# Stick-breaking attention with queries on partitions, a running product along keys, and weights transposed by DMA

## The reference

```
mask = s_idx[None, :] < t_idx[:, None]
log_keep = jnp.where(mask, jax.nn.log_sigmoid(-z), 0.0)
log_stick = lax.cumsum(log_keep, axis=3, reverse=True) - log_keep
w = jnp.where(mask, jnp.exp(jax.nn.log_sigmoid(z) + log_stick), 0.0)
outs.append(jnp.einsum('bhqk,bhkd->bhqd', w.astype(v.dtype), vb))
```

## Time and profile before

| | us |
|---|---|
| runs of the kernel | 2827.84, 2835.94 and 3204.79; median 2835.94 |
| span of the profiled execution, slowest core (core 1) | 2821.7 |
| spans of the 8 cores in it | 2811.3 to 2821.7 |
| what lies around the span: median less span | 14.2 |
| what lies around the span: lowest run less span | 6.1 |

### The profile page before, as it was taken

The page is one execution under the profiler, slowest core; times in us unless marked ns, Lnnn a source line. Parts: engine busy times, 40 slices in busy tenths (PEclk is TensorE's granted clock), DMA queues, the critical chain, the costliest instruction groups (busy, mean ns, idle before and its releaser), DMA issues.

```text
span 2821.7 us, 37239 instructions; the slowest of 8 cores (2811.3 to 2821.7 us)
## 1 busy us (share of the span) xinstructions
PE 2501.4 (89%) x12740; PEld 1036.7 (37%) x12740; DVE 1023.9 (36%) x1602; ACT 1201.3 (43%) x1559; POOL 69.6 (2%) x88
## 2 busy tenths in 40 slices
PE   3988788788999899999998888778899999999993
PEld 1433232222444344444444332222234444444441
DVE  3223232222344543343442332222233364343343
ACT  4346778787223211111343576788842231111132
POOL 0000000000000000000000000000000000000000
PEclk9999798888999999999999998888899999999997
DMA  6110020000222222205002001100022433330202
GB/s 160 16 16 1 1 31 1 1 1 12 27 38 38 45 46 45 46 1 77 1 1 31 1 1 19 12 1 1 1 28 33 53 45 45 45 44 12 36 30 90
DMA packets 79829, 79.81 MB, mean 28 GB/s; under 512 B 4128, under 2 KB 65696, under 8 KB 79648
## 3 DMA queue, kind: packets, MB, share of 16 engines
q0 software_dynamic: 69696, 60.54, 15.6%
q1 hardware_dynamic: 9952, 16.89, 1.8%
HBM read 129.57 MB, written 8.39 MB: 49 GB/s over the span
## 4 chain that ended last, share of the span: by engine, by line
PE 80%; ACT 8%; DVE 4%; DMA 4%; issue 3%; ACTq 0%; DVEq 0%; SPq 0%; POOLq 0%
PE psb L245 58%; PE psb L252 20%; ACT BW L261 5%; PE psb L248 3%; DMA X<-xT 2%; ACT L261 1%; DVE MIX L264 1%; DMA yT<-BW 1%; DVE BW L277 1%; ACT FW L261 1%; DVE H L267 1%; DVE BW L274 0%; DMA WB<-w_in 0%; DVE MIX L274 0%; DMA WB<-w_out 0%
## 5 line engine op out<-in xcount | busy, mean ns | idle before, releaser
L261 ACT ACTIVATE FW<-psb 128x512 f32<-128x512 f32 (+7 forms) x509 | 370.8, 742 | 932.0 <-PE psb L245 795.8
L245 PE MATMUL psb<-H,MIX 128*128 128x512 bf16 (+1 forms) x3168 | 630.7, 358 | 0.5 <-DVE MIX L264 0.3
L252 PE MATMUL psb<-BW,CST 128*128 128x512 bf16 (+5 forms) x1352 | 381.5, 399 | 38.4 <-DVE BW L264 38.4
L245 PEld LDWEIGHTS psb<-H,MIX 128*128 128x128 bf16 x3168 | 286.0, 98 | 336.7 <-issue 7.5
L252 PE MATMUL psb<-MIX 64*128 64x512 bf16 (+5 forms) x1424 | 274.0, 389 | 127.7 <-ACT BW L261 123.0
L261 ACT ACTIVATE BW<-psb 128x1024 bf16<-128x1024 f32 (+5 forms) x424 | 354.8, 904 | 52.3 <-PE psb L252 50.4
L264 DVE TENSOR_TENSOR X<-X,psb 128x512 f32<-128x512 f32 (+1 forms) x504 | 307.9, 629 | 146.3 <-PE psb L245 145.7
L245 PE MATMUL psb<-MIX 128*128 128x512 bf16 (+1 forms) x1584 | 327.9, 357 | 31.8 <-DVE MIX L264 31.5
L264 DVE TENSOR_TENSOR BW<-BW 128x1024 bf16<-128x1024 bf16 (+2 forms) x320 | 195.5, 611 | 367.9 <-PE psb L252 211.2
L245 PE MATMUL psb<-H,WB 128*128 128x512 bf16 (+1 forms) x1472 | 313.5, 364 | 1.3 <-ACT FW L261 0.8
L264 DVE TENSOR_TENSOR MIX<-FW,psb 128x512 bf16<-128x512 f32 (+1 forms) x198 | 124.1, 630 | 452.4 <-PE psb L245 449.3
(11 more groups left out here) (47 smaller groups left out, 1140.2 us busy)
## 6 DMA issues: line engine op xcount, KB each, us to landing
MIX<-w_ffn_in POOLq DMA_DIRECT2D x20, 1024.0 KB, 14.0
MIX<-w_ffn_out POOLq DMA_DIRECT2D x10, 1024.0 KB, 22.4
X<-xT SPq DMA_DIRECT2D x4, 2048.0 KB, 35.1
WB<-w_in POOLq DMA_DIRECT2D x8, 1024.0 KB, 20.0
yT<-BW SPq DMA_DIRECT2D x32, 256.0 KB, 2.5
WB<-w_in POOLq DMA_DIRECT2D x12, 512.0 KB, 8.5
WB<-w_out POOLq DMA_DIRECT2D x4, 1024.0 KB, 10.9
BW<-w_in POOLq DMA_DIRECT2D x4, 512.0 KB, 9.6
```

Source lines behind the costliest of these rows:

```text
L245: P.op('pe', lambda e: e.matmul(out, lhsT=lhsT, rhs=rhs, start=start, stop=stop), reads, writes, inc)
L252: P.op('pe', lambda e: e.matmul(out, lhsT=lhsT, rhs=rhs, start=start, stop=stop, skip_group_check=True), reads, writes, inc)
L261: P.op('act', lambda e: e.activation(out=out, in_=in_, func=func, **kw), reads, writes)
```

## The change

Tokens are laid out in reversed order (the host reverses x and the learned tokens, and reverses the output back), so that keys before a query lie to the right of it. Attention is written anew with queries on partitions. A unit is one head, one block of 128 queries and up to eight key blocks. For each unit TensorE computes z (one or two matmuls of up to 457 columns, and a mask on the diagonal), ScalarE computes sigmoid(-z) into float32, which is 1 - beta, VectorE runs `tensor_tensor_scan` along the keys, which leaves the running product, and subtracts neighbouring columns of it, which gives the weights in bf16. A longer key prefix is cut into two or three chunks, and one column of the product is copied as the start of the next. Then the SP queue transposes the weights block by block with `dma_start_transpose`, SBUF to SBUF, and TensorE multiplies them with V, for two query blocks and two heads together.

Softplus, Exp, the second z, the triangular matmul and the running sum go. The tiles WB, BW and FW become parts of one tile ATT, which attention uses whole. So k and v are projected for all tiles before attention, and the first merge slab is loaded after it. There are 232 units in the first layer and 224 in the second.

```diff
@@ token order and key blocks @@
-TT = [(0, 16)] + [(16 + 512 * i, 16 + 512 * (i + 1)) for i in range(4)]
-KB = [(0, 16)] + [(16 + 128 * j, 144 + 128 * j) for j in range(16)]
+TT = [(512 * i, 512 * (i + 1)) for i in range(4)] + [(2048, 2064)]
+KB = [(128 * j, 128 * j + 128) for j in range(16)] + [(2048, 2064)]
...
@@ memory: one tile ATT now holds what WB, BW and FW were @@
-        FW = sb("FW", 2048, F32)
+        ATT = sb("ATT", 20480, BF16)
-        WB = sb("WB", 4 * 2048, BF16)
-        BW = sb("BW", 8192, BF16)
+        WB, BW, FW = Sub(ATT, 0), Sub(ATT, 8192), Sub(ATT, 16384, 2)
+        P.alias = dict(WB=('ATT', 0, 1), BW=('ATT', 8192, 1), FW=('ATT', 16384, 2))
...
@@ attention: all of the former body removed @@
-        def attention(work=None, after_work=None, ft=0):
...
+        def chunks(b):
+            n = 17 - b
+            nch = 1 if n <= 8 else 2 if n <= 15 else 3
+            cuts, k = [], b
+            for c in range(nch):
+                m = -(-(17 - k) // (nch - c))
+                if c < nch - 1:
+                    m = min(m, 7)
+                cuts.append((k, k + m))
+                k += m
+            return cuts
+
+        def attention(l, ft=0):
+            KE0, WR0, WT0 = 0, 6144, 10240
+            memset('dve', MIX[:, 8256:8272], 0.0, [('MIX', 8256, 8272)])
+            memset('pool', ATT[:, WR0:WR0 + 4096], 0.0, [('ATT', WR0, WR0 + 4096)])
+            units, nch, npo = [], 0, 0
+            for g in ([8] if ft == 0 else []) + list(range(7, -1, -1)):
+                bs = [16] if g == 8 else [2 * g, 2 * g + 1]
+                for hp in range(4):
+                    chs = chunks(bs[0])
+                    for ci, (ka, kz) in enumerate(chs):
+                        ch = dict(bs=bs, hp=hp, ka=ka, kz=kz, first=ci == 0, last=ci == len(chs) - 1,
+                                  wt=WT0 + (nch % 2) * 4096, po=6 + npo % 2)
+                        nch += 1
+                        for bi, b in enumerate(bs):
+                            lo = max(ka, b)
+                            if lo >= kz:
+                                continue
+                            for hh in range(2):
+                                units.append(dict(ch=ch, bi=bi, b=b, hh=hh, lo=lo, end=False, n=len(units)))
+                        units[-1]['end'] = True
+                    npo += 1
+
+            def geo(u):
+                k0, k1 = KB[u['lo']][0], KB[u['ch']['kz'] - 1][1]
+                return k0, k1, k1 - k0 + 2, KB[u['b']][1] - KB[u['b']][0]
+
+            def ke(u):
+                return KE0 + (u['n'] % 3) * 2048
+
+            def zap(u, nq, W):
+                T_ = PSB[u['n'] % 3]
+                if W <= 512:
+                    return T_[0:nq, 0:W]
+                return T_[0:nq, :].rearrange("p (h c) -> p h c", h=2)[:, :, 0:W // 2]
+
+            def prep(u):
+                k0, k1, W, nq = geo(u)
+                ch, hp, hh = u['ch'], u['ch']['hp'], u['hh']
+                q0 = KB[u['b']][0]
+                T_, zb = PSB[u['n'] % 3], 2 * (u['n'] % 3)
+                p0, p1 = 64 * hh, 64 * hh + 64
+                diag = u['lo'] == u['b']
+                parts = [(0, W)] if W <= 512 else [(0, W // 2), (W // 2, W)]
+                mw = min(NMSK, W)
+                for x, (a, b_) in enumerate(parts):
+                    msk = diag and x == 0
+                    mmx(T_[0:nq, x * 512:x * 512 + b_ - a], Q.ap(hp, q0, q0 + nq, p0, p1),
+                        K.ap(hp, k0 - 2 + a, k0 - 2 + b_, p0, p1), True, not msk,
+                        [Q.r(hp, q0, q0 + nq), K.r(hp, k0 - 2 + a, k0 - 2 + b_)], [psr(zb + x)], not msk)
+                    if msk:
+                        mmx(T_[0:nq, 0:mw], CST[0:nq, 0:nq], CST[0:nq, 128:128 + mw], False, True,
+                            [r_cst], [psr(zb)], True)
+
+            def core(u):
+                k0, k1, W, nq = geo(u)
+                ch = u['ch']
+                L = W - 2
+                kb_ = ke(u)
+                r_ke = ('ATT', kb_, kb_ + 2 * W)
+                E = ATT[0:nq, kb_:kb_ + 2 * W].bitcast(F32)
+                out = E if W <= 512 else E.rearrange("p (h c) -> p h c", h=2)
+                zb = 2 * (u['n'] % 3)
+                act(out, zap(u, nq, W), AF.Sigmoid, [psr(zb)] + ([psr(zb + 1)] if W > 512 else []), [r_ke],
+                    scale=-1.0)
+                cs = u['bi'] * 2 + u['hh']
+                init = 1.0 if u['lo'] == u['b'] else CAR[0:nq, cs:cs + 1]
+                r_car = ('CAR', cs * 16, cs * 16 + 16)
+                P.op('dve', lambda e: e.tensor_tensor_scan(
+                    out=E, data0=E, data1=ZF[0:nq, 0:1].to_broadcast([nq, W]), initial=init,
+                    op0=ALU.mult, op1=ALU.add),
+                    [r_ke, ('ZF', 0, 16)] + ([] if u['lo'] == u['b'] else [r_car]), [r_ke])
+                if not ch['last']:
+                    cp('dve', CAR[0:nq, cs:cs + 1], E[:, W - 3:W - 2], [r_ke], [r_car])
+                wo = WR0 + (u['n'] % 4) * 1024
+                r_w = ('ATT', wo, wo + 1024)
+                tt(SUBE, ATT[0:nq, wo:wo + L], E[:, 1:L + 1], E[:, 2:L + 2], ALU.subtract, [r_ke], [r_w])
+                nb = ch['kz'] - u['lo']
+                wt = ch['wt']
+                W4 = ATT[:, wt:wt + 4096].rearrange("p (k h q) -> p k h q", h=2, q=256)
+                i0 = u['lo'] - ch['ka']
+                qc = u['bi'] * 128
+                dst = W4[:, i0:i0 + nb, u['hh'], qc:qc + nq]
+                src = ATT[0:nq, wo:wo + nb * 128]
+                wr = [('ATT', wt + (k * 2 + u['hh']) * 256 + qc, wt + (k * 2 + u['hh']) * 256 + qc + nq)
+                      for k in range(i0, i0 + nb)]
+                P.dma('sp', lambda e: e.dma_start_transpose(out=dst, in_=src), 'tw%d' % (u['n'] % 4), [r_w], wr)
+
+            def av(ch):
+                hp, po, wt = ch['hp'], ch['po'], ch['wt']
+                for kb in range(ch['ka'], ch['kz']):
                     b0, b1 = KB[kb]
+                    nk = b1 - b0
+                    i0 = kb - ch['ka']
+                    N = sum(KB[b][1] - KB[b][0] for b in ch['bs'] if b <= kb)
+                    st_ = ch['first'] and i0 == 0
+                    sp_ = ch['last'] and kb == ch['kz'] - 1
                     for hh in range(2):
...
@@ the order of a layer @@
             ecnt = [0]
-            if ft == 0:
-                proj_fm(l, 0, 0, 'q')
-            proj_fm(l, 1, 0, 'q')
-            for i in range(5):
+            for i in (4, 3, 2, 1, 0):
+                if i in tl:
+                    proj_fm(l, i, 0, 'q')
                 proj_u(l, i, 2, ecnt)
-                if i + 2 < 5:
-                    proj_fm(l, i + 2, 0, 'q')
-                if i == 2:
-                    load_in_slab(l, 512, 0)
-                if i >= ft:
+                if i in tl:
                     pool_band(l, i)
+            load_in_slab(l, 512, 0)
             load_in_slab(l, 1024, 2)
-            for i in range(2):
+            for i in (4, 3, 2, 1, 0):
                 proj_fm(l, i, 0, 'k')
-            for i in range(2):
                 proj_v(l, i, 2)
-            work = {}
-            for i in range(1, 4):
-                work[i] = proj_fm_items(l, i + 1, 0, 'k', eng='dve') + proj_v_items(l, i + 1, 2)
-            attention(work, after_work=lambda l=l: load_merge_slab(l, 0), ft=ft)
+            attention(l, ft)
+            load_merge_slab(l, 0)
             sgcnt = [0]
...
-        m["xT"] = f(x[b].T)
+        m["xT"] = f(x[b][::-1].T)
```

More of the change, by code:

```diff
@@ L40, in __init__, with _res @@
         self.arenas = {}
+        self.alias = {}
     def arena(self, name, nelem):
         self.arenas[name] = dict(n=(nelem + CELL - 1) // CELL, W={}, R={})
+    def _res(self, rs):
+        out = []
+        for (an, lo, hi) in rs:
+            if an in self.alias:
+                an, off, mul = self.alias[an]
+                lo, hi = off + lo * mul, off + hi * mul
+            out.append((an, lo, hi))
+        return out
     def _record(self, eng, fn, reads, writes, stream, val, skip):
         need = {}
+        reads, writes = self._res(reads), self._res(writes)
         for (an, lo, hi) in reads:
@@ L630, in merge_slab @@
-        def merge_slab(l, j, sgcnt, ft=0):
+        def chunks(b):
[93 more added lines that the diff above has]
+                for kb in range(ch['ka'], ch['kz']):
+                    b0, b1 = KB[kb]
+                    nk = b1 - b0
[3 more added lines that the diff above has]
+                    sp_ = ch['last'] and kb == ch['kz'] - 1
+                    for hh in range(2):
+                        h = 2 * hp + hh
+                        o_ = wt + (i0 * 2 + hh) * 256
+                        out, lh, rh = (PS[po][64 * hh:64 * hh + 64, 0:N], V.ap(kb, h * 64, h * 64 + 64, 0, nk),
+                                       ATT[0:nk, o_:o_ + N])
+                        P.op('pe', lambda e, out=out, lh=lh, rh=rh, st_=st_, sp_=sp_, hh=hh: e.matmul(
```

(30 more changed lines are left out.)

294 lines of the change are left out of this document (77 added, 217 removed).

## The result

The changed kernel takes 3015.84 us (median of its runs, 3012.46 to 3082.40) beside 2833.24 for the kernel before: a ratio of 1.065, 95% interval 1.063 to 1.068. The forecast was 3025 us, slower with 0.86.

A forecast was written before the change was run, and what follows sets the result against it. Attention was taken as a tight exchange of TensorE and ScalarE, with VectorE binding after the change. Layers of +93 and +96 us made 2821.7 + 189 = 3011, plus 14.2 around the span: 3025 us; 8-in-10 range 2790 to 3620.

The forecast's parts named there:

- The bound: Attention stage: after the change VectorE's summed work sets its length, 556 us in the first layer and 553 in the second.
- The scan at two passes: VectorE in attention: the scan costs 2.084 ns per column, 332 us in the first layer and 331 in the second.
- Subtractions: VectorE in attention: neighbouring columns subtracted at 1.042 ns per column and 158 ns fixed, 184 us in the first layer.
- Copies: VectorE in attention: 96 small copies of the carried column per layer at 175 ns, 17 us.
- Dependent starts: VectorE in attention: an instruction reading the result before it starts 0.10 us late; 232 such starts, 23 us.
- TensorE and ScalarE: Attention, first layer: at most 424 us of TensorE and 180 of ScalarE, covered by VectorE and costed at nothing.
- k and v ahead: Before attention: 192 projection matmuls per layer no longer hidden, 41.5 us, plus 8.5 us of weight loads.
- Exit: End of attention: the first merge slab's weights load only once attention's buffers are free, 9 us (0 to 12).
- End of the second attention: Second layer: attention 37 us longer, with another 9 us for loading the first merge slab's weights.
- Transposes: SP's queue in attention: landing in 2.5 us like the store, hidden except latency of 15 and 5 us per layer.
- Around the span: Outside the profiled span: 14.2 us added to reach the median of the runs shown.
- A price among the rivals: Scan at the subtraction's pace: 2729 us, said to stay below 2779 up to about 1.45 ns per column; chance 0.07.

## Why the prediction was right, point by point

- **The bound.** VectorE's list sets the end of attention: shown by the waits, by the run without the chain, and by the run without subtractions.
- **The scan at two passes**: 332 us in the first layer, measured 336.4 (189.3 + 147.1); 1.23 us for 514 columns, measured 1.22. The section of the Trainium skill on the datapath of VectorE (DVE: opcode table, instruction layouts, handler registers and perf-mode slots, section 6), which gives the scan half throughput, is borne out by 2.083 ns against 1.042. The prediction's own reason, that each column needs the one to its left, stays an argument: no run parts the chain from the addition.
- **Subtractions** 184 us, measured 184.0. **Copies** 17, measured 14.8.
- **Dependent starts**: taken as 0.10 us each, 23 us; a subtraction that waits for scan and buffer starts 0.17 us late, and these with the copies make 34. Against that, instructions in a row overlap by some 0.08 us, which the forecast did not have: durations sum to 536 us, VectorE's busy time is 513. One term is 11 us too small, another of 23 us is missing; the list with its starts comes to 547 us for 556 forecast.
- **TensorE and ScalarE** were costed at nothing, with 424 us for TensorE as a bound from rows at a clock of 0.85. The granted clock fell to 0.50, which the prediction did not foresee; TensorE was busy for 283 us all the same, and VectorE covered it.
- **k and v ahead**: +50 per layer forecast, +49.5 and +46.7 measured. The size is right, the words were not: "what attention no longer hides" suggests free work made visible. The kernel before with k and v hoisted shows that they had cost almost the same inside. Among the signs the prediction named some 52 us for k and v, which its own sum does not give: 17.0 and 50 make 67, and 66.5 and 63.3 were measured.
- **Exit**: 9 us forecast; +14.7 in the first layer. The term was priced by the landing of one 512 KB load, 7.8 us; the first tile of 16 tokens needs all four loads of the slab at once, and the last of them landed 16 us after the last value product.
- **End of the second attention**: +37.4 for 46 with the exit. VectorE was done 549 us after the start, earlier than its list said, and then 10.5 us went into the wait for the last transpose, which took 11.4 us to land. It is the only one of this core's 456 over 5 us, and the first load of the merge's weights had been issued 1.6 us ahead of it; in the first layer that load came 0.5 us behind the last transpose, which landed in 2.6. So the agreement of this row with the 37 alone is luck.
- **Transposes**: hidden, with 2.7 us to landing where the store's 2.5 was taken. The estimate from the Trainium skill (VectorE: DVE Perf Modes, The three transpose paths) of 1309 ns for each 128 by 128 would be some 6.9 us for the mean unit of 5.3 blocks. The trace shows 1.2 us of issue and 2.7 to landing for a whole unit, and with doubled transposes 464 passed in 667 us. So the measurement decides against scaling that figure by blocks.
- **Not foreseen**: 13 us elsewhere. At the start the clearing of the ones shares a cell with the constants and waits for their DMA (2.7 us in the run that took it away); the rest of the +8.1 and +10.4 was not tried one by one.
- **Around the span**: 14.2 us forecast, 1.9 measured (3016.40 less 3014.5). The forecast took a median and a span from different executions of the kernel before; beside its own span a run of it is 1.5 us longer (2825.70 and 2824.2 in one). So the span came out 4 us over the forecast and the part around it 12 us under.
- **A price among the rivals** was summed wrongly: from 2729 us, the time stays below 2779 up to about 1.22 ns per column of the scan; at the 1.45 named there it would be some 2845. The forecast does not use it.

What decided direction and size, the scan's rate and VectorE's whole list, was argued and came true. That the total lies within 10 us is partly luck, since errors of 4 to 23 us went either way.

## What to carry to other kernels

When work moves to an engine that looks idle, add up its whole list before counting what the others are spared: here 390 us free became 513 busy out of 573. An instruction whose columns depend on one another should be priced at two passes until a row shows otherwise; this case has one such instruction. And look for the algebra that takes a pass away from the new bound: a subtraction moved from each weight to V, once per layer, turned a loss of 6.5% into a gain of 3.2%, and copies that wait two units longer made it 4.4%.

## What was not expected of the hardware

Subtractions on GpSimd and scans on VectorE take turns: a scan of 770 columns takes 2499 ns beside them and 1754 without, and a subtraction of 656 columns 2.49 us inside a scan and 1.27 when it starts first. A transpose of up to eight key blocks costs 1.2 us of SP's queue, and one follows another after 1.33 us in a full queue, which is reached before the data path is. TensorE's clock was granted at 0.50, the 1.2 GHz level, through both attentions, where TensorE was busy for 283 of 573 us; in the windows of k and v just ahead it was 0.92 and 0.97.
